# Feed-forward products as pairs of 64-row matmuls in two PSUM banks

## The chip, the cores and the metric

One core of a Trainium2 chip runs the kernel. The metric is the device time in microseconds from the first to the last instruction, the median of several runs. One more execution is recorded by the hardware profiler; all rows below come from it.

## What is computed

One layer of a hybrid encoder block in float32, 256 tokens of width 2048: a combined input projection, latent attention and a convolution branch, a gated merge, cross-attention to 256 memory tokens, a SwiGLU feed-forward of width 5632, and a final RMSNorm. The change touches only the feed-forward part:

```python
def rms_norm(x, g):
    xf = x.astype(jnp.float32)
    y = xf * lax.rsqrt(jnp.mean(xf * xf, axis=-1, keepdims=True) + EPS)
    return (y * g.astype(jnp.float32)).astype(x.dtype)

def swiglu(h, w_gate, w_up, w_down):
    return (jax.nn.silu(h @ w_gate) * (h @ w_up)) @ w_down
...
        x = x + swiglu(rms_norm(x, norm_ffn[l]), w_gate[l], w_up[l], w_down[l])
    return rms_norm(x, norm_final)
```

## The kernel before

The kernel is a hand-written program for each engine, synchronised by semaphores; nothing plans it at run time. All large products are done in split form: a float32 operand is a sum of two fp32r parts, high and low, and a product of two operands is three matmuls (low x high, high x low, high x high) that add into the same PSUM bank. The activations are kept transposed in SBUF as such pairs (crossT, actT: 128 rows of the contraction, 16 or 44 blocks, 256 tokens).

The weights come from memory in tiles of 128 rows x 2 blocks x 512 columns (512 KB). Tile t goes through a ring of four places: SyncE loads it into `raw` (`tile`, L259, waits until `split_lo` is done with the place's last tile), ScalarE rounds it to w_hi (`split_hi`, L717; it waits for the DMA and, for tile t, until TensorE is done with tile t - 4), VectorE subtracts to w_lo (`split_lo`, L1162), TensorE multiplies (`products`, L324). In the streams of ScalarE and VectorE the split of tile t + 4 stands at step t.

A chunk is 512 columns of the output for all 256 tokens. It lies in `acc`, two banks, one for each block b of 128 tokens. `products` does for one weight tile: for b in 0, 1, for each block k of the tile, three matmuls of 128 x 128 against 128 x 512. A full tile is thus 12 matmuls. A chunk of gate or up is 8 tiles, a chunk of down 24 tiles (four of them with one block: 264 matmuls). On the chunk's last tile the end of block 0 is signalled by `acc0_full`, the end of block 1 by `tile_done`, six matmuls later. On the first tile of a chunk the matmuls of block b wait for `acc_free[b]`.

The feed-forward stage has 11 pairs of chunks (gate, up), the first written out, ten in a loop (L689), then four chunks of down (L698). The counts are 176 x 12 = 2112 matmuls for gate and up and 4 x 264 = 1056 for down. ScalarE evicts a gate chunk with the silu (`silu_out`, L1103, the output silu_g is the first half of row_bc, so the profile calls it row_bc) ahead of its split of step 7. VectorE evicts an up chunk (`gated_up`, L1555: acc times rfac times silu_g, to `stage`) ahead of its split of step 14. After tile 1 of the next pair TensorE transposes `stage` (`turn_stage`, L354: eight 128x128 transposes in fp32 against the identity) and the two engines take the result apart into actT (`act_hi`, `act_lo`). VectorE evicts a down chunk by adding acc to the residual xs (L1593), ahead of its split of step 22; ScalarE then sums the squares (L748). The PSUM banks `sc` are used by the attention parts and are idle in the feed-forward stage.

In the attention part, at L452 and L457, scores are made in fp32: per head, 128-row products with 128 and 256 columns into bank sc[:, h], then the rope part with only 64 rows of contraction. The two heads' rope parts lie in partitions 0:64 and 64:128. An fp32 matmul call shows as two passes in the trace.

Of the kernel before, what the change touches and what calls it, by code (L numbers as in the profile page):

```python
# [23 lines left out]
ACT = mybir.ActivationFunctionType  # L24
ALU = mybir.AluOpType
# [3 lines left out]
P = 128  # L29
TOK = 256  # L30
NB = TOK // P
D = 2048
DK = D // P
CH = 512
# [5 lines left out]
D_FF = 5632  # L40
# [7 lines left out]
RING = 4  # L48
# [37 lines left out]
def program(nc, x, mem, positions, norm_mix, w_in, b_conv_in, norm_cq, w_uq, norm_ckv, w_ukv, w_dw,  # L86
# [15 lines left out]
    with ctx:  # L102
# [3 lines left out]
        def sem(name):  # L106
            return ctx.enter_context(nc.semaphore(name))
# [127 lines left out]
        silu_done = sem("silu_done")  # L235
        x_done = sem("x_done")
        table_loaded = sem("table_loaded")
        gained = sem("gained")
# [81 lines left out]
        def _(pe):  # L320
# [3 lines left out]
            def products(base, t, n_tiles, lhs, k0, kt, n, chunk):  # L324

                s = t % RING
                first, last = t == 0, t == n_tiles - 1
                pe.wait_ge(lo_done, base + (t + 1))
                for b in range(NB):
                    if first and not (isinstance(chunk, int) and chunk == 0):  # L330
                        pe.wait_ge(acc_free[b], chunk)
                    for k in range(kt):
                        hi = lhs[0][:, k0 + k, b * P:(b + 1) * P]
                        lo = lhs[1][:, k0 + k, b * P:(b + 1) * P]
                        whi = w_hi[:, s, k * n:(k + 1) * n]
# [5 lines left out]
                        ins = mm(o, hi, whi, start=False, stop=end)  # L341
                    if last and b == 0:
                        ins.then_inc(acc0_full, 1)
                ins.then_inc(tile_done, 1)
# [336 lines left out]
            for t in range(8):  # L681
                if t % 2 == 0:
                    operand_ready(Q_H + t // 2)
                products(T_I, t, 8, crossT, 2 * t, 2, CH, C_I)
                if t == 1:
                    turn_stage(Q_H + 3, 2 * (S_H + 4))
            for t in range(8):
                products(T_I + 8, t, 8, crossT, 2 * t, 2, CH, C_I + 1)
            with pe.Fori(1, D_FF // CH) as i:  # L689
                for t in range(8):  # L690
                    products(i * 16 + T_I, t, 8, crossT, 2 * t, 2, CH, 2 * i + C_I)
                    if t == 1:
                        turn_stage(i + (Q_I - 1), 2 * i + 2 * S_I)
                for t in range(8):
                    products(i * 16 + (T_I + 8), t, 8, crossT, 2 * t, 2, CH, 2 * i + (C_I + 1))


            def down(c, first):  # L698
                for t in range(24):
                    k, kt = down_tile(t)  # L700
                    if first and t == 22:
                        operand_ready(Q_I + 10)
                    products(c * 24 + T_J, t, 24, actT, k, kt, CH, c + C_J)
                    if first and t == 1:
                        turn_stage(Q_I + 10, 2 * (S_I + 11))

# [7 lines left out]
        def _(act):  # L714
            fn = nc.scalar.activation

            def split_hi(base, t, width=TW):  # L717

                s = t % RING
                act.wait_ge(raw_full[s], base * 4 + (16 * (t // RING) + 16))  # L720
                if not (isinstance(base, int) and base + t < RING):
                    act.wait_ge(tile_done, base + (t - RING + 1))
                fn(w_hi[:, s, 0:width], raw[:, s, 0:width], ACT.Copy).then_inc(hi_done, 1)  # L723
# [376 lines left out]
                x_update(c, False, T_H, Q_H, S_H, Z_H, R_FFN, "norm_ffn")  # L1100


            def silu_out(chunk, last_tile, n):  # L1103

                if not (isinstance(n, int) and n == 0):
                    act.wait_ge(stage_full, 2 * n + 2 * S_I)
                for b in range(NB):
                    acc_full(b, chunk, last_tile)
                    fn(silu_g[:, b, :], acc[:, b, :], ACT.Silu, scale=rfac[:, R_FFN, b:b + 1])\
                        .then_inc(silu_done, 1)  # L1110
                    act.wait_ge(silu_done, 2 * n + (b + 1))
                    act.sem_inc(acc_free[b], 1)

            def act_hi(n, count):
                for g in range(2):
                    turned_hi_part(g, count + (g + 1), [actT[0][:, cols(n * 4 + 2 * g, 2), :]])

            for t in range(16):
                if t == 7:
                    act.wait_ge(r_ready, R_FFN + 1)  # L1120
                    silu_out(C_I, T_I + 8, 0)
                split_hi(T_I, t + 4)
                if t == 1:
                    new_x_hi(3, crossT, "norm_ffn", 2 * (Q_H + 3))
                    load_table(ACT.Silu)
            with act.Fori(1, D_FF // CH) as i:
                for t in range(16):
                    if t == 7:
                        silu_out(2 * i + C_I, i * 16 + (T_I + 8), i)
                    split_hi(i * 16 + T_I, t + 4)  # L1130
                    if t == 1:
                        act_hi(i - 1, 2 * i + (2 * Q_I - 2))


            def down(c, first, end):
                for t in range(24):
                    if t + 4 < 24 or not end:
                        split_hi(c * 24 + T_J, t + 4, down_tile((t + 4) % 24)[1] * CH)
                    if first and t == 1:
                        act_hi(10, 2 * (Q_I + 10))  # L1140
                for b in range(NB):
                    act.wait_ge(x_done, 2 * c + (b + 1))
                    sum_squares(2 * c + (Z_J + b), R_FIN, b, c, xs[:, b, cols(c * CH, CH)])
# [15 lines left out]
        def _(dve):  # L1159
# [10 lines left out]
            def acc_full(b, chunk, last_tile):  # L1170
                if b == 0:
                    dve.wait_ge(acc0_full, chunk + 1)
                else:
                    dve.wait_ge(tile_done, last_tile)
# [377 lines left out]
                        new_x_lo(c - 1, "norm_ffn", 2 * c + (H_H - 2))  # L1552


            def gated_up(b, n, chunk, last_tile, free):  # L1555

                dve.wait_ge(turned, free)
# [11 lines left out]
            for t in range(16):  # L1569
                if t == 0:  # L1570
                    mean_square(R_FFN, D, 4, Z_H + 8)
                if t == 14:
                    dve.wait_ge(x_new, 8)
                    dve.wait_ge(r_ready, R_FFN + 1)
                for b in range(NB) if t == 14 else ():
                    gated_up(b, 0, C_I + 1, T_I + 16, 2 * (Q_H + 4))
                split_lo(T_I, t + 4)
                if t == 1:
                    new_x_lo(3, "norm_ffn", H_H + 6)
            with dve.Fori(1, D_FF // CH) as i:  # L1580
                for t in range(16):
                    for b in range(NB) if t == 14 else ():
                        gated_up(b, i, 2 * i + (C_I + 1), i * 16 + (T_I + 16), 2 * i + 2 * Q_I)
                    split_lo(i * 16 + T_I, t + 4)
                    if t == 1:
# [211 lines left out]
```

## Time and profile before

| what | value |
|---|---|
| median of 3 runs | 1701.45 us (1700.97 to 1701.63) |
| profiled execution | 1700.04 us, its span 1698.2 us |
| TensorE busy | 1679.2 us, 7808 matmuls |
| VectorE busy | 972.7 us |
| ScalarE busy | 814.0 us |
| feed-forward, gate and up | 958.5 to 1447.5 us of the span |
| feed-forward, down | 1447.5 to 1687.8 us |

PE is TensorE's matmuls, PEld its weight loads, DVE VectorE, ACT ScalarE, SP SyncE. A row of the timeline gives the start and the length in us, then engine, line, operation, output and inputs. A matmul's length is a modelled one from the start of its reading to its end, longer than the distance to the next matmul, which starts meanwhile. A group of instructions of one form that follow each other is one row with its count.

### The profile page before, as it was taken

How to read it: one execution, taken by the hardware profiler on the slowest of the kernel's cores; microseconds unless marked ns; L12 is line 12 of the kernel's file. 1: busy time of each engine (PE TensorE's matmuls, PEld its weight loads, DVE VectorE, ACT ScalarE, POOL GpSimd, SP SyncE). 2: the span in 40 equal slices, each digit the busy share in tenths (PEclk: the TensorE clock that was granted, in tenths of full speed). 3: DMA queues.
4: the chain of work that ended last, by engine and by line, in shares of the span. 5: the costliest groups of instructions: out<-in, count | busy, mean ns of one | idle time of the engine just before them, and what ended most of it. 6: DMA issues, size and time to landing. Idle time of an engine off the chain costs nothing.

```text
span 1698.2 us, 23828 instructions
## 1 busy us (share of the span) xinstructions
PE 1679.2 (99%) x7808; PEld 1393.2 (82%) x7808; DVE 972.7 (57%) x1154; ACT 814.0 (48%) x1061; POOL 88.0 (5%) x154
## 2 busy tenths in 40 slices
PE   8999999999999999999999999999999999999997
PEld 6888888888888888888778888888888888888886
DVE  5545777778886467554445645544444454554453
ACT  6555555556545444445445544444444444344343
POOL 4100100010000000000000000000000000000000
PEclk9999999999999999999999999999999999999999
DMA  6866555555566655554435566666666666565563
GB/s 214 273 195 170 170 164 152 166 155 167 173 210 186 197 174 179 193 187 148 135 124 186 186 187 190 192 188 188 182 184 197 195 188 187 197 211 186 183 212 124
DMA packets 161295, 309.64 MB, mean 182 GB/s; under 512 B 10323, under 2 KB 16577, under 8 KB 160992
## 3 DMA queue, kind: packets, MB, share of 16 engines
q1 hardware_dynamic: 159168, 302.55, 57.9%
q0 software_dynamic: 1776, 6.47, 1.0%
q8 instruction: 27, 0.44, 0.1%
q14 instruction: 20, 0.16, 0.0%
q10 hardware_dynamic: 304, 0.01, 0.0%
HBM read 306.89 MB, written 2.10 MB: 182 GB/s over the span
## 4 chain that ended last, share of the span: by engine, by line
PE 98%; ACT 1%; DMA 0%; DVE 0%; issue 0%; ACTq 0%; POOL 0%; DVEq 0%
PE acc L339 29%; PE acc L341 29%; PE acc L340 29%; PE tp L351 3%; PE sc L631 1%; PE acc L530 1%; PE sc L452 1%; PE acc L532 1%; PE acc L531 1%; PE ov L650 0%; PE acc L510 0%; PE acc L512 0%; PE acc L511 0%; PE ov L476 0%; PE xt L650 0%; PE sc L457 0%
## 5 line engine op out<-in xcount | busy, mean ns | idle before, releaser
L1167 DVE TENSOR_TENSOR w_lo<-raw,w_hi 128x1024 fp32r<-128x1024 f32 (+3 forms) x592 | 709.9, 1204 | 606.1 <-ACT w_hi L723 602.3
L723 ACT ACTIVATE w_hi<-raw 128x1024 fp32r<-128x1024 f32 (+3 forms) x592 | 606.8, 1027 | 786.8 <-PE acc L341 751.7
L339 PE MATMUL acc<-w_hi,crossT 128*128 128x512 f32 x832 | 327.4, 394 | 0.0
L341 PE MATMUL acc<-w_hi,crossT 128*128 128x512 f32 x832 | 324.1, 390 | 0.0
L340 PE MATMUL acc<-w_lo,crossT 128*128 128x512 f32 x832 | 323.9, 389 | 0.0
L339 PE MATMUL acc<-w_hi,mixT 128*128 128x512 f32 x800 | 318.2, 398 | 2.9 <-DVE w_lo L1167 2.4
L341 PE MATMUL acc<-w_hi,mixT 128*128 128x512 f32 x800 | 312.8, 391 | 0.0
L340 PE MATMUL acc<-w_lo,mixT 128*128 128x512 f32 x800 | 312.6, 391 | 0.0
L339 PEld LDWEIGHTS acc<-w_hi,crossT 128*128 128x128 f32 x832 | 156.2, 188 | 32.8 <-issue 0.7
L341 PEld LDWEIGHTS acc<-w_hi,crossT 128*128 128x128 f32 x832 | 156.2, 188 | 32.7
L340 PEld LDWEIGHTS acc<-w_lo,crossT 128*128 128x128 f32 x832 | 156.3, 188 | 32.2 <-issue 0.7
L339 PEld LDWEIGHTS acc<-w_hi,mixT 128*128 128x128 f32 x800 | 150.8, 188 | 37.4 <-issue 6.4
L341 PEld LDWEIGHTS acc<-w_hi,mixT 128*128 128x128 f32 x800 | 150.7, 188 | 32.0
L340 PEld LDWEIGHTS acc<-w_lo,mixT 128*128 128x128 f32 x800 | 151.0, 189 | 29.4
L339 PE MATMUL acc<-w_hi,actT 128*128 128x512 f32 x352 | 137.0, 389 | 0.0
L341 PE MATMUL acc<-w_hi,actT 128*128 128x512 f32 x352 | 136.9, 389 | 0.0
L340 PE MATMUL acc<-w_lo,actT 128*128 128x512 f32 x352 | 136.9, 389 | 0.0
L1291 DVE SCALAR_TENSOR_TENSOR conv<-uT,wdwT,conv (+1 forms) x240 | 118.2, 492 | 19.5 <-DVE conv L1291 16.7
L341 PEld LDWEIGHTS acc<-w_hi,actT 128*128 128x128 f32 x352 | 66.1, 188 | 13.8
L339 PEld LDWEIGHTS acc<-w_hi,actT 128*128 128x128 f32 x352 | 66.1, 188 | 13.7
L340 PEld LDWEIGHTS acc<-w_lo,actT 128*128 128x128 f32 x352 | 66.1, 188 | 13.6
L339 PE MATMUL acc<-w_hi,oT 128*128 128x512 f32 x128 | 51.0, 399 | 0.1
(224 smaller groups left out, 1235.1 us busy)
## 6 DMA issues: line engine op xcount, KB each, us to landing
raw<-in_w_in_dram SPq DMA_DIRECT2D x104, 512.0 KB, 3.8
raw<-in_w_gate_dram SPq DMA_DIRECT2D x88, 512.0 KB, 4.5
raw<-in_w_up_dram SPq DMA_DIRECT2D x88, 512.0 KB, 3.7
raw<-in_w_down_dram SPq DMA_DIRECT2D x80, 512.0 KB, 4.0
raw<-in_w_kv_mem_dram SPq DMA_DIRECT2D x64, 512.0 KB, 3.8
raw<-in_w_o_dram SPq DMA_DIRECT2D x32, 512.0 KB, 3.9
raw<-in_w_q_mem_dram SPq DMA_DIRECT2D x32, 512.0 KB, 3.6
raw<-in_w_o_mem_dram SPq DMA_DIRECT2D x32, 512.0 KB, 3.6
```

What stands on the lines that cost most here:

```text
L339: mm(o, lo, whi, start=first and k == 0, stop=False)
L340: mm(o, hi, wlo, start=False, stop=False)
L341: ins = mm(o, hi, whi, start=False, stop=end)
L351: ins = turn(tp[:, bank, j * P:(j + 1) * P], src, ident[:, :])
L452: mm(sc[:, h, at:at + keys], qnT[:, h, qs:qs + P], knT[:, h, 0:keys], start=qs == 0, stop=False, skip_group_check=True)
L530: mm(o, lo, w_hi[:, s, k * n:(k + 1) * n], start=first and k == 0, stop=False)
L531: mm(o, hi, w_lo[:, s, k * n:(k + 1) * n], start=False, stop=False)
L532: ins = mm(o, hi, w_hi[:, s, k * n:(k + 1) * n], start=False, stop=last and k == kt - 1)
L631: ins = mm(sc[:, 0, b * TOK:(b + 1) * TOK], memqT[:, k, b * P:(b + 1) * P], memKT[:, cols(h * 4 + k, 1), :].rearrange("p o t -> p (o t)"), ...
L723: fn(w_hi[:, s, 0:width], raw[:, s, 0:width], ACT.Copy).then_inc(hi_done, 1)
L1167: V.tensor_tensor(w_lo[:, s, 0:width], raw[:, s, 0:width], w_hi[:, s, 0:width].bitcast(F32), ALU.subtract).then_inc(lo_done, 1)
L1291: ins = V.scalar_tensor_tensor(out=a, in0=u, scalar=wt, in1=a, op0=ALU.mult, op1=ALU.add)
```

## The change

In the whole feed-forward stage `products` is replaced by `half_products`: each 128-row matmul becomes two of 64 rows, the upper half of the contraction into acc[:, b], the lower into sc[:, b]; the two are issued one behind the other. An output is then the sum of two banks. At eviction ScalarE copies the half in sc to SBUF (`half_copy`, into silu_g for a gate chunk, into `stage` for the others), VectorE adds acc to it in place (`gate_sum`, `gated_up`, and in `down`), and that addition signals `acc_free`. The silu then runs in place in SBUF behind ScalarE's split of step 7, the product with rfac and silu_g (`gated`) in SBUF behind VectorE's split of step 14, and the addition to xs as a second addition. In the down chunks `half_copy` stands behind ScalarE's split of step 23.

```diff
+            def half_products(base, t, n_tiles, lhs, k0, kt, chunk):
+
+                s = t % RING
+                first, last = t == 0, t == n_tiles - 1
+                pe.wait_ge(lo_done, base + (t + 1))
+                for b in range(NB):
+                    if first:
+                        pe.wait_ge(acc_free[b], chunk)
+                    for k in range(kt):
+                        hi, lo = lhs[0][:, k0 + k, b * P:(b + 1) * P], lhs[1][:, k0 + k, b * P:(b + 1) * P]
+                        whi, wlo = w_hi[:, s, k * CH:(k + 1) * CH], w_lo[:, s, k * CH:(k + 1) * CH]
+                        for n, (a, w) in enumerate(((lo, whi), (hi, wlo), (hi, whi))):
+                            for bank, rows in ((acc, slice(0, 64)), (sc, slice(64, P))):
+                                ins = mm(bank[:, b, :], a[rows, :], w[rows, :], start=first and k == 0 and n == 0,
+                                         stop=last and k == kt - 1 and n == 2)
                     if last and b == 0:
                         ins.then_inc(acc0_full, 1)
                 ins.then_inc(tile_done, 1)
...
             with pe.Fori(1, D_FF // CH) as i:
                 for t in range(8):
-                    products(i * 16 + T_I, t, 8, crossT, 2 * t, 2, CH, 2 * i + C_I)
+                    half_products(i * 16 + T_I, t, 8, crossT, 2 * t, 2, 2 * i + C_I)
                     if t == 1:
                         turn_stage(i + (Q_I - 1), 2 * i + 2 * S_I)
...
-            def silu_out(chunk, last_tile, n):
-
-                if not (isinstance(n, int) and n == 0):
-                    act.wait_ge(stage_full, 2 * n + 2 * S_I)
+            def half_copy(dst, chunk, last_tile):
+
                 for b in range(NB):
                     acc_full(b, chunk, last_tile)
-                    fn(silu_g[:, b, :], acc[:, b, :], ACT.Silu, scale=rfac[:, R_FFN, b:b + 1])\
+                    fn(dst[:, b, :], sc[:, b, :], ACT.Copy).then_inc(half_out, 1)
+
+            def silu_out(chunk):
+
+                for b in range(NB):
+                    act.wait_ge(acc_free[b], chunk + 1)
+                    fn(silu_g[:, b, :], silu_g[:, b, :], ACT.Silu, scale=rfac[:, R_FFN, b:b + 1])\
                         .then_inc(silu_done, 1)
-                    act.wait_ge(silu_done, 2 * n + (b + 1))
-                    act.sem_inc(acc_free[b], 1)
...
             with act.Fori(1, D_FF // CH) as i:
                 for t in range(16):
                     if t == 7:
-                        silu_out(2 * i + C_I, i * 16 + (T_I + 8), i)
+                        act.wait_ge(stage_full, 2 * i + 2 * S_I)
+                        half_copy(silu_g, 2 * i + C_I, i * 16 + (T_I + 8))
+                    if t == 15:
+                        act.wait_ge(turned, 2 * i + 2 * Q_I)
+                        half_copy(stage, 2 * i + (C_I + 1), i * 16 + (T_I + 16))
                     split_hi(i * 16 + T_I, t + 4)
+                    if t == 7:
+                        silu_out(2 * i + C_I)
...
                         split_hi(c * 24 + T_J, t + 4, down_tile((t + 4) % 24)[1] * CH)
                     if first and t == 1:
                         act_hi(10, 2 * (Q_I + 10))
+                    if t == 23:
+                        if first:
+                            act.wait_ge(turned, 2 * (Q_I + 11))
+                        act.wait_ge(x_done, 2 * c)
+                        half_copy(stage, c + C_J, c * 24 + (T_J + 24))
...
+            def gated_up(b, n):
+
+                dve.wait_ge(half_out, 4 * n + (b + 3))
+                V.tensor_tensor(stage[:, b, :], acc[:, b, :], stage[:, b, :], ALU.add).then_inc(acc_free[b], 1)
+
+            def gated(b, n, chunk):
+
+                dve.wait_ge(acc_free[b], chunk + 1)
                 dve.wait_ge(silu_done, 2 * n + (b + 1))
-                acc_full(b, chunk, last_tile)
-                V.scalar_tensor_tensor(out=stage[:, b, :], in0=acc[:, b, :], scalar=rfac[:, R_FFN, b:b + 1],
+                V.scalar_tensor_tensor(out=stage[:, b, :], in0=stage[:, b, :], scalar=rfac[:, R_FFN, b:b + 1],
                                        in1=silu_g[:, b, :], op0=ALU.mult, op1=ALU.mult).then_inc(stage_full, 1)
-                dve.wait_ge(stage_full, 2 * n + (2 * S_I + b + 1))
-                dve.sem_inc(acc_free[b], 1)
+
+            def gate_sum(b, n):
+
+                dve.wait_ge(half_out, 4 * n + (b + 1))
+                V.tensor_tensor(silu_g[:, b, :], acc[:, b, :], silu_g[:, b, :], ALU.add).then_inc(acc_free[b], 1)
...
             with dve.Fori(1, D_FF // CH) as i:
                 for t in range(16):
+                    for b in range(NB) if t == 6 else ():
+                        gate_sum(b, i)
                     for b in range(NB) if t == 14 else ():
-                        gated_up(b, i, 2 * i + (C_I + 1), i * 16 + (T_I + 16), 2 * i + 2 * Q_I)
+                        gated_up(b, i)
                     split_lo(i * 16 + T_I, t + 4)
+                    for b in range(NB) if t == 14 else ():
+                        gated(b, i, 2 * i + (C_I + 1))
...
                         acc_full(b, c + C_J, c * 24 + (T_J + 24))
-                        V.tensor_tensor(xs[:, b, cols(c * CH, CH)], acc[:, b, :], xs[:, b, cols(c * CH, CH)],
+                        dve.wait_ge(half_out, 2 * c + (4 * (D_FF // CH) + b + 1))
+                        V.tensor_tensor(stage[:, b, :], acc[:, b, :], stage[:, b, :], ALU.add).then_inc(acc_free[b], 1)
+                        dve.wait_ge(acc_free[b], c + (C_J + 1))
+                        V.tensor_tensor(xs[:, b, cols(c * CH, CH)], stage[:, b, :], xs[:, b, cols(c * CH, CH)],
                                         ALU.add).then_inc(x_done, 1)
-                        dve.wait_ge(x_done, 2 * c + (b + 1))
-                        dve.sem_inc(acc_free[b], 1)
```

## Rows read from the trace of the kernel before

**Rows 1.** The page: busy time, the clock granted in 40 slices, the chain.

```profile
PE 1679.2 (99%) x7808; PEld 1393.2 (82%) x7808; DVE 972.7 (57%) x1154; ACT 814.0 (48%) x1061; POOL 88.0 (5%) x154
...
PEclk9999999999999999999999999999999999999999
...
PE 98%; ACT 1%; DMA 0%; DVE 0%; issue 0%; ACTq 0%; POOL 0%; DVEq 0%
```

**Rows 2.** Groups by line, TensorE, feed-forward stage: count, busy us, mean ns, idle.

```profile
L339 PE MATMUL acc<-w_hi,crossT 128*128 128x512 f32 x704 | 274.9, 391 | 0.0
...
L339 PE MATMUL acc<-w_hi,actT 128*128 128x512 f32 x352 | 137.0, 389 | 0.0
```

**Rows 3.** Timeline, TensorE, down products: the first and the last of 15.

```profile
1579.66 0.39 PE L339 MATMUL acc<-w_hi,actT 128*128 128x512 f32 x1
...
1582.84 0.39 PE L341 MATMUL acc<-w_hi,actT 128*128 128x512 f32 x1
```

**Rows 4.** Timeline, products of 384 columns: the first and the last of 12.

```profile
237.08 0.33 PE L531 MATMUL acc<-w_lo,cqT 128*128 128x384 f32 x1
...
238.98 0.33 PE L530 MATMUL acc<-w_hi,cqT 128*128 128x384 f32 x1
```

**Rows 5.** Timeline, TensorE, scores: whole stretch, then windows that cut the half passes.

```profile
218.36 0.38 PE L452 MATMUL sc<-knT,qnT 128*128 128x256 f32 x1
...
218.67 0.93 PE L457 MATMUL sc<-krT,qrT 64*128 64x128 f32 x8
219.53 0.50 PE L339 MATMUL acc<-w_hi,mixT 128*128 128x512 f32 x1
219.86 0.40 PE L340 MATMUL acc<-w_lo,mixT 128*128 128x512 f32 x1
...
218.67 0.38 PE L457 MATMUL sc<-krT,qrT 64*128 64x128 f32 x2
...
218.67 0.49 PE L457 MATMUL sc<-krT,qrT 64*128 64x128 f32 x4
...
219.00 0.59 PE L457 MATMUL sc<-krT,qrT 64*128 64x256 f32 x3
```

**Rows 6.** Timeline, TensorE, the transposes of `stage` between products.

```profile
1052.68 0.39 PE L341 MATMUL acc<-w_hi,crossT 128*128 128x512 f32 x1
1052.91 1.03 PE L351 MATMUL tp<-ident,stage 128*128 128x128 f32 x8
...
1054.02 0.39 PE L340 MATMUL acc<-w_lo,crossT 128*128 128x512 f32 x1
```

**Rows 7.** Timeline, the end of a gate chunk and its eviction.

```profile
1068.55 0.39 PE L341 MATMUL acc<-w_hi,crossT 128*128 128x512 f32 x1
...
1068.98 0.69 ACT L1109 ACTIVATE row_bc<-acc,rfac 128x512 f32<-128x512 f32 x1 [0.30 <-PE acc L341]
...
1069.91 0.39 PE L341 MATMUL acc<-w_hi,crossT 128*128 128x512 f32 x1
1069.91 0.19 PEld L339 LDWEIGHTS acc<-w_hi,crossT 128*128 128x128 f32 x1
```

**Rows 8.** Groups by line, ScalarE and VectorE, feed-forward stage.

```profile
L736 ACT ACTIVATE actT<-tp 128x512 f32 x20 | 10.7, 588 | 0.0
...
L1593 DVE TENSOR_TENSOR xs<-acc,xs 128x512 f32<-128x512 f32 x4 | 2.8, 692 | 10.2 <-PE acc L341 10.2
```

**Rows 9.** Timeline, the end of the first down chunk.

```profile
1508.04 0.39 PE L341 MATMUL acc<-w_hi,actT 128*128 128x512 f32 x1
...
1508.52 1.06 ACT L723 ACTIVATE w_hi<-raw 128x1024 fp32r<-128x1024 f32 x1 [1.66 <-PE acc L341]
```

**Rows 10.** Timeline, behind the last matmul.

```profile
1687.56 0.39 PE L341 MATMUL acc<-w_hi,actT 128*128 128x512 f32 x1
...
1687.98 0.69 DVE L1593 TENSOR_TENSOR xs<-acc,xs 128x512 f32<-128x512 f32 x1 [0.67 <-PE acc L341]
1688.70 0.63 ACT L748 ACTIVATE junk<-xs 128x512 f32<-128x512 f32 x1 [0.64 <-DVE xs L1593]
```

More of the change, by code:

```diff
@@ L234, in program @@
         x_new = sem("x_new")
-        silu_done = sem("silu_done")
+        silu_done, half_out = sem("silu_done"), sem("half_out")
         x_done = sem("x_done")
@@ L341, in products @@
                         ins = mm(o, hi, whi, start=False, stop=end)
+                    if last and b == 0:
+                        ins.then_inc(acc0_full, 1)
+                ins.then_inc(tile_done, 1)
+            def half_products(base, t, n_tiles, lhs, k0, kt, chunk):
[12 more added lines that the diff above has]
+                                         stop=last and k == kt - 1 and n == 2)
                     if last and b == 0:
@@ L683, in _ @@
                     operand_ready(Q_H + t // 2)
-                products(T_I, t, 8, crossT, 2 * t, 2, CH, C_I)
+                half_products(T_I, t, 8, crossT, 2 * t, 2, C_I)
                 if t == 1:
@@ L687, in _ @@
             for t in range(8):
-                products(T_I + 8, t, 8, crossT, 2 * t, 2, CH, C_I + 1)
+                half_products(T_I + 8, t, 8, crossT, 2 * t, 2, C_I + 1)
             with pe.Fori(1, D_FF // CH) as i:
                 for t in range(8):
-                    products(i * 16 + T_I, t, 8, crossT, 2 * t, 2, CH, 2 * i + C_I)
+                    half_products(i * 16 + T_I, t, 8, crossT, 2 * t, 2, 2 * i + C_I)
                     if t == 1:
@@ L694, in _ @@
                 for t in range(8):
-                    products(i * 16 + (T_I + 8), t, 8, crossT, 2 * t, 2, CH, 2 * i + (C_I + 1))
+                    half_products(i * 16 + (T_I + 8), t, 8, crossT, 2 * t, 2, 2 * i + (C_I + 1))
             def down(c, first):
@@ L702, in down @@
                         operand_ready(Q_I + 10)
-                    products(c * 24 + T_J, t, 24, actT, k, kt, CH, c + C_J)
+                    half_products(c * 24 + T_J, t, 24, actT, k, kt, c + C_J)
                     if first and t == 1:
@@ L1119, in _ @@
                 if t == 7:
+                    half_copy(silu_g, C_I, T_I + 8)
+                if t == 15:
+                    act.wait_ge(turned, 2 * (Q_H + 4))
+                    half_copy(stage, C_I + 1, T_I + 16)
+                split_hi(T_I, t + 4)
+                if t == 7:
                     act.wait_ge(r_ready, R_FFN + 1)
-                    silu_out(C_I, T_I + 8, 0)
-                split_hi(T_I, t + 4)
+                    silu_out(C_I)
                 if t == 1:
@@ L1128, in _ @@
                     if t == 7:
-                        silu_out(2 * i + C_I, i * 16 + (T_I + 8), i)
+                        act.wait_ge(stage_full, 2 * i + 2 * S_I)
+                        half_copy(silu_g, 2 * i + C_I, i * 16 + (T_I + 8))
+                    if t == 15:
+                        act.wait_ge(turned, 2 * i + 2 * Q_I)
+                        half_copy(stage, 2 * i + (C_I + 1), i * 16 + (T_I + 16))
                     split_hi(i * 16 + T_I, t + 4)
+                    if t == 7:
+                        silu_out(2 * i + C_I)
                     if t == 1:
@@ L1574, in _ @@
                     dve.wait_ge(r_ready, R_FFN + 1)
+                for b in range(NB) if t == 6 else ():
+                    gate_sum(b, 0)
                 for b in range(NB) if t == 14 else ():
-                    gated_up(b, 0, C_I + 1, T_I + 16, 2 * (Q_H + 4))
+                    gated_up(b, 0)
                 split_lo(T_I, t + 4)
+                for b in range(NB) if t == 14 else ():
+                    gated(b, 0, C_I + 1)
                 if t == 1:
@@ L1581, in _ @@
                 for t in range(16):
+                    for b in range(NB) if t == 6 else ():
+                        gate_sum(b, i)
                     for b in range(NB) if t == 14 else ():
-                        gated_up(b, i, 2 * i + (C_I + 1), i * 16 + (T_I + 16), 2 * i + 2 * Q_I)
+                        gated_up(b, i)
                     split_lo(i * 16 + T_I, t + 4)
+                    for b in range(NB) if t == 14 else ():
+                        gated(b, i, 2 * i + (C_I + 1))
                     if t == 1:
```

2 lines of the change are left out of this document (removed).

## Prediction

> **What bounds the kernel now.** I read the page first: TensorE is busy for 1679.2 of 1698.2 us, its clock is at full level in every slice, and it holds 98% of the chain that ended last [rows 1]. So the time is the number of matmuls times their pitch, plus whatever makes TensorE wait. In the feed-forward stage the groups of instructions by line show no idle time in front of any matmul group: 3 lines x 704 with crossT and 3 x 352 with actT, 3168 products of 128x512 [rows 2]. The reported 390 ns of one is a modelled length that overlaps the next one, so I take the pitch from the timeline: 14 steps from 1579.66 to 1582.84 us are 0.227 us each [rows 3]. 3168 x 0.227 = 719 us; 12 groups of 8 transposes add 10. That is the whole stage: it has no slack and no waits, and anything added to TensorE's path is paid in full. The 384-wide products take 0.173 (11 steps in 1.90 us [rows 4]): 128 columns less save 0.054 us, 0.42 ns each, one column per cycle of 2.4 GHz. So of the 0.227 us, 0.213 are columns and 0.0135 a fixed part.
>
> **Pitch of a pair.** Each product of 128 rows becomes two of 64 rows on the two halves of the array, into acc and sc: 6336 matmuls and 6336 weight loads for the same arithmetic. A half streams the same 512 columns, so a pair can at best cost what one product costs now. Whether the two run side by side is shown by the rope part of the attention scores, which already does exactly this (rows 0:64 and 64:128, banks sc 0 and sc 1). In its timeline two matmuls start within the same 0.01 us, the next two 0.11 later than the first work could begin (4 done at 218.67 + 0.49), and with 256 columns the third starts at 219.00 + 0.59 - 0.38 = 219.21, about 0.22 after the first of its pair [rows 5]. For whole-array fp32 the transposes give 0.109 for 128 columns [rows 6], so about 0.216 for 256. So a pair costs what a single one costs, within a rounding of 1 to 3 ns. What this does not show is the 1-pass fp32r form at a full column per cycle and its 13.5 ns fixed part (in fp32 a column takes two cycles, and of the 0.109 only 2 ns are fixed). Bounds: the fixed part disappears for halves, 0.227 - 0.011 = 0.216, or is paid once for each half, 0.227 + 0.0135 = 0.2405. The nearest row (the half pairs) says "the same", so I take +1 ns: 3168 x 0.001 = **+3 us**, with -35 and +43 us as ends.
>
> In the Trainium skill, the page "TensorE: Matmul & The Clock Gate" (Part 3, The mechanism) models a pack as one matmul's duration plus about 4 ns per further tile. No 512-column pair is in this trace; as an estimate by that page the term would be 3168 x 0.004 = 13 us in place of 3, and the total 1736.
>
> **Changing between whole array and halves.** The last full pass of the scores starts at 218.36, the half passes last 2 x 0.11 + 2 x 0.22 = 0.66, so without any loss the next two full products would start at 219.24 and 219.47. The second one starts at 219.86 [rows 5]: 0.39 to 0.40 us for an excursion, 0.20 per change. In the changed stage the excursion goes the other way: the transposes of turn_stage are whole-array. They come 12 times (one in the first gate chunk, ten in the loop, one in the first down chunk), plus one entry into the stage: 25 changes x 0.20 = 5.0 us. Today the same transposes lose next to nothing: 1052.68 + 0.227 + 8 x 0.109 + 0.227 = 1054.01 against 1054.02 seen [rows 6]. **+4.9 us.**
>
> **Freeing the accumulator, gate and up chunks.** Before, one instruction reads acc[b] and frees it. Take M, the start of the last matmul of block 0 of a chunk (1068.55). ScalarE starts at M + 0.43, and TensorE's weight load for the next chunk's block 0 comes at M + 1.36 [rows 7]; the present silu of 0.69 ends in time by 0.2. After the change ScalarE copies the sc half (0.59 us, as the actT copy of the same 128x512 out of PSUM), and only then VectorE adds (0.69 us, as the x add of the same shape) [rows 8], with 0.03 us from one engine to the next (1687.98 + 0.69 to 1688.70 [rows 10]). So the bank is free at M + 0.43 + 0.59 + 0.03 + 0.69 + 0.03 = M + 1.77, 0.41 after the weight load wanted it. A weight load may be 0.12 late for free, since it needs no more than 0.109 of the 0.227. Stall: 0.30 us (0.29 rounded up). Block 1's copy starts 1.36 later and its add is over at M + 3.14, when its weight load, itself pushed to M + 2.72 + 0.30, may wait until 3.14: no second stall. There are 11 gate-to-up, 10 up-to-gate and one up-to-down boundaries: 22 x 0.30 = **+6.6 us**. VectorE and ScalarE are otherwise free then; what queues behind their waits is split_lo(t+4) and split_hi(t+4), due three tiles or 8 us later. The silu in SBUF and the product with rfac come after the bank is free: on no path, except that the next turn_stage needs both some 5.4 us after the chunk's end. I find them done at 4.5 (add 1.8, split_lo 1.25, two products of 0.75 at most). If that cover failed, each of 11 turn_stages would wait for the excess.
>
> **Freeing it in the down chunks.** Here half_copy stands behind split_hi(27), and that waits for the last tile of the chunk. With M1 the start of the chunk's very last matmul (1508.04), the split starts at M1 + 0.48 and takes 1.06 [rows 9]; then copy of block 0 to M1 + 2.15, add to 2.87, seen at 2.90, while the next chunk's weight load wants to go at M1 + 0.00. Less the free 0.12: 2.78 us of stall, at 3 boundaries **+8.3 us**. Block 1 follows within its 1.36 us. The splits of tiles 26 and 27 end by M1 + 7.6, their use is at 8.4 and later.
>
> **Tail.** Before, the last x add runs from M1 + 0.42 for 0.69 [rows 10], over at 1.11. After: copy to 1.01, VectorE still has block 0's second add until 1.09, then two adds of 0.69 with 0.03 each in front, over at 2.53. **+1.4 us.**
>
> Sum: 3 + 4.9 + 6.6 + 8.3 + 1.4 = 24.4 us. The profiled execution took 1700.0, so it would take 1724.4; the median lies 1.4 above that execution, which gives **1726 us**.
>
> **Rivals.**
> 1. *The fixed part is paid by every half* (the two halves share what costs 13.5 ns between matmuls). For it: nothing in the trace has fp32r halves, and two loads and two matmuls now pass where one each did. Against: in the rope pairs it was not doubled [rows 5]. Pitch 0.2405, +43 us in place of +3; the boundary stalls shrink a little. About 1765.
> 2. *The halves hide the weight change*, and the fixed part goes. The page "TensorE: Matmul & The Clock Gate" in the Trainium skill gives 512/2.4 + 2.5 ns, 216 ns, as back-to-back gap (Back-to-back issue gap), and says that a weight load overlaps running matmuls only where the row group differs (Part 3); by that rule the change would gain. Against: a load starts with the running whole-array matmul already now (both at 1069.91 [rows 7]), and both halves change weights at the same moment, so neither covers the other. Worked out from rows: -35 + 21.2 = -14 us at full effect, 1688; at half effect 1705. This is how it ends faster: it decides once the pair's pitch falls below 0.227 - 21.2/3168 = 0.2203.
> 3. *The pairs don't run side by side* in this form, because two banks would now take a full column per cycle each, twice what the rope pairs wrote. Pitch 0.454, about +720 us: 2440. A part of it (one half delayed by some tens of ns) would land between.
> 4. *More stalls than counted*: three gaps of 2.8 us in the down chunks let the clock fall to 1.2 GHz (no fall is seen within the stage now [rows 1]); if each then slowed one tile of 2.7 us to half speed, +8 us; or transposes wait for the later products. About 1735 to 1745.
>
> **How the numbers follow.** Forecast (pitch 0.226 to 0.230): 0.58, its own range 1721 to 1735. Rival 1: 0.14. Rival 2: 0.14, of which 0.09 faster by over 0.2%, 0.03 within it and 0.02 slower. Rival 3: 0.06. Rival 4: 0.08. A measurement of this kernel can tell about 0.2% (3.4 us) from no change. Faster 0.09, within 0.2% 0.04 (the 0.03 and a hundredth for stalls that vanish with an unchanged pitch), slower 0.87. The range 1704 to 1770 takes in the forecast, rivals 1 and 4 and the weak end of rival 2, and leaves out the serial case and the clear gain.
>
> **What the profile after would show.** Right: some 6336 half matmuls of 64 rows, two starting together and the next two 0.228 later; about 0.3 us of TensorE waiting for VectorE at each of 22 boundaries, 2.8 at three; 0.2 more in front of and behind each group of 8 transposes. Wrong: a pitch near 0.240 or 0.216 (rival 1 or 2), second halves starting 0.2 behind the first (rival 3), a digit below 9 in the clock's row (rival 4), or boundaries without idle time, which would mean that the copy or the add is shorter than the rows taken for them, or that TensorE's wait is later than its weight load.

## The result

The changed kernel takes 1725.7 us (median of 4 runs, 1724.8 to 1727.6) against 1701.2 us before on the same chip: a ratio of 1.0148, 95% interval 1.0136 to 1.0160. It is slower by 24.5 us; 1726 was forecast. The profiled execution took 1724.8 us, its span is 1723.0.

The page of the kernel after, to be held against [rows 1]: TensorE's share falls by one point although it now has 10976 matmuls, and the chain goes through VectorE and ScalarE at times.

```profile
span 1723.0 us, 30227 instructions
...
PE 1692.7 (98%) x10976; PEld 1398.0 (81%) x10976; DVE 1003.7 (58%) x1206; ACT 840.2 (49%) x1113; POOL 87.2 (5%) x154
...
PE 95%; ACT 2%; DVE 1%; DMA 1%; issue 1%; ACTq 0%; POOL 0%; DVEq 0%; SPq 0%
```

The timeline of TensorE inside a tile, to be held against [rows 3] and [rows 5]: two halves start together, the next two 0.227 us later (7 steps in 1.59 us). The pairs run side by side in fp32r as the rope parts did in fp32.

```profile
1399.83 0.39 PE L359 MATMUL acc<-w_hi,crossT 64*128 64x512 f32 x1
1399.84 0.39 PE L359 MATMUL sc<-w_hi,crossT 64*128 64x512 f32 x1
1400.06 0.39 PE L359 MATMUL acc<-w_lo,crossT 64*128 64x512 f32 x1
...
1401.42 0.39 PE L359 MATMUL acc<-w_lo,crossT 64*128 64x512 f32 x1
```

An up-to-gate boundary, all engines, the counterpart of [rows 7] (gate-to-up ones look the same). M is 1048.26. The copy starts at M + 0.43, the addition at M + 1.06; the weight load that could have gone at 1049.62 goes at 1050.07, M + 1.81. Of these 0.45 us the free 0.12 of the prediction goes off, and 0.33 is lost:

```profile
1048.26 0.39 PE L359 MATMUL sc<-w_hi,crossT 64*128 64x512 f32 x1
...
1048.69 0.60 ACT L1126 ACTIVATE stage<-sc 128x512 f32<-128x512 f32 x1 [0.30 <-PE sc L359]
...
1049.32 0.69 DVE L1595 TENSOR_TENSOR stage<-acc,stage 128x512 f32<-128x512 f32 x1 [2.39 <-ACT stage L1126]
...
1049.62 0.39 PE L359 MATMUL acc<-w_hi,crossT 64*128 64x512 f32 x1
...
1050.07 0.18 PEld L359 LDWEIGHTS acc<-w_hi,crossT 64*128 64x128 f32 x1 [0.48 <-DVE stage L1595]
```

The first down boundary, counterpart of [rows 9]: the chunk's last matmul starts at 1521.01, the split runs first, then two copies (one row), then the addition, and the next chunk begins at 1523.90. The two steps that are stretched come to 2.89 + 0.34, which is 2.77 more than two steps of 0.227.

```profile
1521.01 0.39 PE L359 MATMUL acc<-w_hi,actT 64*128 64x512 f32 x1
...
1521.50 1.06 ACT L742 ACTIVATE w_hi<-raw 128x1024 fp32r<-128x1024 f32 x1 [1.66 <-PE sc L359]
1522.47 1.06 ACT L1126 ACTIVATE stage<-sc 128x512 f32<-128x512 f32 x2
1523.15 0.69 DVE L1646 TENSOR_TENSOR stage<-acc,stage 128x512 f32<-128x512 f32 x1 [4.76 <-ACT stage L1126]
...
1523.90 0.49 PE L359 MATMUL acc<-w_hi,actT 64*128 64x512 f32 x1 [2.50 <-DVE stage L1646]
```

The transposes of `stage`, counterpart of [rows 6]. From the last pair in front to the second pair behind there are 1057.12 - 1055.45 = 1.67 us; two steps of 0.227 and eight of 0.109 are 1.33, so 0.35 is lost (before: 0.01).

```profile
1055.45 0.39 PE L359 MATMUL acc<-w_hi,crossT 64*128 64x512 f32 x1
...
1055.77 1.09 PE L370 MATMUL tp<-ident,stage 128*128 128x128 f32 x8
1056.79 0.50 PE L359 MATMUL acc<-w_hi,crossT 64*128 64x512 f32 x1
...
1057.12 0.39 PE L359 MATMUL acc<-w_lo,crossT 64*128 64x512 f32 x1
```

And one thing that no step of the sum had: behind the second of the three long gaps the clock fell. The busy time by stretches (columns: stretch and length in us, then TensorE, weight loads, VectorE, ScalarE, GpSimd, then the granted clock, the share of the DMA engines and GB/s) shows the gap, the stretch behind it, and the one after that:

```profile
1583.90:1586.40 2.50, 0.15 (x2) 0.00 (x0) 0.69 (x1) 2.03 (x3) 0.00 (x0) 1.00 0.51 179
1586.40:1590.90 4.50, 4.48 (x26) 3.56 (x28) 4.23 (x5) 1.45 (x4) 1.22 (x1) 0.62 0.00 0
1590.90:1595.40 4.50, 4.50 (x42) 4.07 (x40) 3.88 (x3) 2.12 (x2) 1.19 (x1) 1.00 0.54 167
```

A clock of 0.62 over this stretch is most of it at 1.2 GHz: in the timeline seven steps in a row take 0.427 us each, and the stretch as a whole costs 1.6 us. The page's row of the clock, which the prediction named as the sign, does not show it: it has 9 in every fortieth (43 us) of the stage, and an 8 only in the last one, where the clock fell behind the last product.

**Where the 24.8 us of the span went.** The feed-forward stage, from the start of its first matmul to the start of its last, went from 729.05 to 751.60 us, +22.6. The steps of the timeline in it, taken one by one, give: 22 boundaries of gate and up 7.5 us (19 of 0.33, two of 0.39, one of 0.49), three down boundaries 8.1 (2.77, 2.64, 2.66), 12 groups of transposes and the entry 4.3, the low clock 1.6, and the pitch 1.0 (the steady steps, those beside waits, transposes and the low clock, are 0.2272 us on average against 0.2269). Behind the last matmul it is 1.9 us more, ahead of the stage 0.3.

### The profile page after: what moved, and what is told of

It reads as the page before. It is cut to its first block, busy times and chain, and to the rows that moved or that the text cites. A ratio compares the mean times of both kernels' runs of the same rounds, so it can differ in the third digit from the quotient of the medians.

```text
span 1723.0 us, 30227 instructions
## 1 busy us (share of the span) xinstructions
PE 1692.7 (98%) x10976; PEld 1398.0 (81%) x10976; DVE 1003.7 (58%) x1206; ACT 840.2 (49%) x1113; POOL 87.2 (5%) x154
## 4 chain that ended last, share of the span: by engine, by line
PE 95%; ACT 2%; DVE 1%; DMA 1%; issue 1%; ACTq 0%; POOL 0%; DVEq 0%; SPq 0%
PE acc L359 39%; PE acc L339 15%; PE acc L341 15%; PE acc L340 15%; PE tp L370 3%; PE sc L359 2%; PE sc L650 1%; PE acc L549 1%; PE sc L471 1%; PE acc L551 1%; PE acc L550 1%; ACT stage L1126 1%; PE ov L669 0%; DVE row_bc L1607 0%; DVE stage L1595 0%
## 5 line engine op out<-in xcount | busy, mean ns | idle before, releaser
L359 PE MATMUL acc<-w_hi,crossT 64*128 64x512 f32 x1408 | 441.1, 389 | 1.5 <-DVE stage L1595 0.2
L359 PE MATMUL sc<-w_hi,crossT 64*128 64x512 f32 x1408 | 441.0, 389 | 0.0
L359 PEld LDWEIGHTS acc<-w_hi,crossT 64*128 64x128 f32 x1408 | 259.1, 184 | 67.1 <-DVE stage L1595 5.0
L359 PE MATMUL acc<-w_lo,crossT 64*128 64x512 f32 x704 | 272.1, 387 | 0.0
L359 PE MATMUL sc<-w_lo,crossT 64*128 64x512 f32 x704 | 272.1, 387 | 0.0
L359 PEld LDWEIGHTS sc<-w_hi,crossT 64*128 64x128 f32 x1408 | 259.1, 184 | 1.5
L359 PE MATMUL acc<-w_hi,actT 64*128 64x512 f32 x704 | 218.3, 389 | 7.4 <-DVE stage L1646 7.2
L359 PE MATMUL sc<-w_hi,actT 64*128 64x512 f32 x704 | 218.3, 389 | 0.0
L359 PEld LDWEIGHTS acc<-w_lo,crossT 64*128 64x128 f32 x704 | 129.6, 184 | 24.8
L359 PE MATMUL sc<-w_lo,actT 64*128 64x512 f32 x352 | 136.7, 388 | 0.0
L359 PE MATMUL acc<-w_lo,actT 64*128 64x512 f32 x352 | 136.6, 388 | 0.0
```

Of the source, the lines that this page charges most:

```text
L359: ins = mm(bank[:, b, :], a[rows, :], w[rows, :], start=first and k == 0 and n == 0, stop=last and k == kt - 1 and n == 2)
```

## Experiments

Each ratio is to the kernel before on the same chip; where none is given, the time is that of one execution. The kernel before took 1700.6 to 1701.5 us on these chips, so a difference between two changed kernels can be off by some 0.8 us where they ran on different chips.

**1. The new eviction alone, without halves.** The last matmul of each block of a chunk goes to `sc`, everything behind it is as in the changed kernel:

```diff
-                        for n, (a, w) in enumerate(((lo, whi), (hi, wlo), (hi, whi))):
-                            for bank, rows in ((acc, slice(0, 64)), (sc, slice(64, P))):
-                                ins = mm(bank[:, b, :], a[rows, :], w[rows, :], ...)
+                        end = last and k == kt - 1
+                        mm(acc[:, b, :], lo, whi, start=first and k == 0, stop=False)
+                        mm(acc[:, b, :], hi, wlo, start=False, stop=end)
+                        ins = mm(sc[:, b, :] if end else acc[:, b, :], hi, whi, start=end, stop=end)
```

> Whole-array products as before (the same count of matmuls, no halves, no change between whole array and halves), but the last matmul of each block of a chunk goes to the second bank and the chunk is evicted as in the changed kernel: ScalarE copies the second bank, VectorE adds. Theory (most of the loss is the later freeing of the banks): 22 boundaries x 0.33 us + 3 down boundaries x 2.7 + 1.5 to 2 at the end = 17 us above the kernel before, about 1718, and 1.6 more if the clock falls after one of the long gaps. Rival (the loss is in the half matmuls, their doubled instructions or their loads): nothing of it is here, 1701 to 1704.

Measured: 1722.5 us, ratio 1.0128 (1.0113 to 1.0144), 21.9 us above the kernel before. The mechanism is confirmed: the boundaries have the same stretched steps as with halves (0.445 + 0.335 us in place of twice 0.227; 2.88, 2.75 and 2.75 in the down chunks), and none of what is lost at the boundaries needs half matmuls. The forecast of 1718 was 4 us too low, because here the clock fell at all three long gaps, 4.5 us in all, and not behind one. The pitch tells something too: between the waits the whole-array products of this run take 0.2272 us on average, as the pairs do in the changed kernel.

```profile
1520.00:1522.20 2.20, 2.20 (x7) 1.71 (x6) 2.17 (x4) 1.45 (x4) 0.00 (x0) 0.50 0.00 0
1583.90:1586.90 3.00, 3.00 (x8) 2.32 (x7) 2.84 (x5) 1.45 (x4) 0.37 (x1) 0.50 0.00 0
1648.70:1651.70 3.00, 3.00 (x8) 2.26 (x7) 2.86 (x4) 1.13 (x4) 1.08 (x1) 0.50 0.00 0
```

**2. The copy of the down chunks ahead of the split.**

```diff
                 for t in range(24):
+                    if t == 23:
+                        ...
+                        half_copy(stage, c + C_J, c * 24 + (T_J + 24))
                     if t + 4 < 24 or not end:
                         split_hi(c * 24 + T_J, t + 4, down_tile((t + 4) % 24)[1] * CH)
-                    if t == 23:
-                        ...
-                        half_copy(stage, c + C_J, c * 24 + (T_J + 24))
```

> The changed kernel with the copy of the down chunks placed ahead of ScalarE's split of step 23 instead of behind it. Theory: the three gaps of 2.64 to 2.77 us shrink to the 0.33 of the other boundaries, 7.1 us less, and the 1.6 us at half clock behind one of the gaps go too: 1717 to 1719. Rival (the gap is set by VectorE's two additions per block or by block 1, not by the split ahead of the copy): at most 1 to 2 us less, 1724.

Measured: 1717.3 us, ratio 1.0096 (1.0080 to 1.0111), 8.4 less than the changed kernel. The timeline at the first down boundary: the next chunk begins 0.60 us after 1522.60 in place of 2.89, and ScalarE's split follows the copies. No stretch of the stage is at the low clock any more. So the long gap was the one split of 1.06 us and the missed head start of 1.36 us, not the additions. Of the three boundaries one still costs 0.49 us and two 0.33.

```profile
1521.75 0.60 ACT L1126 ACTIVATE stage<-sc 128x512 f32<-128x512 f32 x1 [0.32 <-PE sc L359]
...
1522.46 0.69 DVE L1646 TENSOR_TENSOR stage<-acc,stage 128x512 f32<-128x512 f32 x1 [1.71 <-ACT stage L1126]
...
1522.60 0.39 PE L359 MATMUL sc<-w_hi,actT 64*128 64x512 f32 x1
...
1523.20 0.50 PE L359 MATMUL acc<-w_hi,actT 64*128 64x512 f32 x1 [0.22 <-DVE stage L1646]
...
1523.52 1.05 ACT L742 ACTIVATE w_hi<-raw 128x1024 fp32r<-128x1024 f32 x1
```

**3 and 4. The price of leaving the halves.** The same extra transpose in each of the 22 gate and up chunks, once in the changed kernel and once in the kernel before:

```diff
+                    if t == 4:
+                        turn(xt[:, 0:P], ident[:, :], ident[:, :])
```

> The changed kernel with one more whole-array transpose of the identity into an unused bank in each of the 22 gate and up chunks (nobody reads it, nothing waits for it). Theory (each change between halves and whole array costs 0.17 to 0.20 us): 22 x (0.109 + 0.34) = 9.9 us more, 1735.6. Rival (the changes are free and the transposes' 1.22 us are something else, a wait for stage or for the bank): 22 x 0.11 = 2.4 us more, 1728.

> The control: the kernel before with the same 22 extra transposes. Both theories: 22 x (0.109 + 0.01) = 2.6 us more, 1704. If it costs 9 us here too, the price is that of a transpose between products and not of changing to halves.

Measured: with halves 1736.6 us (ratio 1.0212, 1.0198 to 1.0226), 10.8 more than the changed kernel without them; whole 1703.6 us (ratio 1.0019, 1.0009 to 1.0028), 2.9 more. In the timeline with halves (the first rows below) the stretch 1020.93 to 1021.84 is 0.91 us, less two steps of 0.227 and 0.109 for the transpose: 0.35 lost per excursion, 7.7 us in 22. With the transposes' 2.4 that is 10.1; the rest of the 10.8 lies in the steady steps (0.2275 us in place of 0.2272). In the control (the last rows) the same place loses 0.007 (0.257 + 0.313). It is the change between halves and whole array that costs, 0.35 there and back. How it divides between the two ways no run shows cleanly; at the entry into the stage, which goes one way only, the two steps are 0.09 and 0.11 us longer than 0.227, 0.20 together.

```profile
1020.93 0.39 PE L359 MATMUL acc<-w_hi,crossT 64*128 64x512 f32 x1
...
1021.25 0.33 PE L716 MATMUL xt<-ident 128*128 128x128 f32 x1
1021.50 0.49 PE L359 MATMUL acc<-w_hi,crossT 64*128 64x512 f32 x1
...
1021.84 0.39 PE L359 MATMUL acc<-w_lo,crossT 64*128 64x512 f32 x1
```

```profile
1017.38 0.39 PE L341 MATMUL acc<-w_hi,crossT 128*128 128x512 f32 x1
1017.61 0.27 PE L697 MATMUL xt<-ident 128*128 128x128 f32 x1
1017.64 0.47 PE L339 MATMUL acc<-w_hi,crossT 128*128 128x512 f32 x1
1017.95 0.40 PE L340 MATMUL acc<-w_lo,crossT 128*128 128x512 f32 x1
```

**5. Three upper halves, then three lower ones.** Is it the alternating order that lets pairs run side by side?

```diff
-                        for n, (a, w) in enumerate(((lo, whi), (hi, wlo), (hi, whi))):
-                            for bank, rows in ((acc, slice(0, 64)), (sc, slice(64, P))):
+                        for bank, rows in ((acc, slice(0, 64)), (sc, slice(64, P))):
+                            for n, (a, w) in enumerate(((lo, whi), (hi, wlo), (hi, whi))):
```

> The changed kernel with the six half matmuls of a block in another order: the three of the upper half, then the three of the lower, in place of alternating. Theory (two halves run side by side only if they follow each other directly, since matmuls start in order): the third upper one runs beside the first lower one and the third lower beside the next first upper, so 4 slots of 0.227 us in place of 3, the feed-forward products take 958 us in place of 719, about 1960 to 1970 in all. Rival (TensorE takes the halves out of order, as it takes weight loads ahead): unchanged, 1726.

Measured: 1727.7 us in one execution, 2 us above the changed kernel's median: the clock fell behind two of its long gaps in place of one, 1.6 us more, and the 22 boundaries of gate and up cost 8.0 in place of 7.5. The 240 us that my theory adds are not there; it was wrong and the rival right. Although the program has three acc matmuls and then three sc matmuls, the timeline shows them in pairs, acc and sc by turns, 0.01 us apart:

```profile
1030.15 0.40 PE L359 MATMUL acc<-w_hi,crossT 64*128 64x512 f32 x1
1030.16 0.40 PE L359 MATMUL sc<-w_hi,crossT 64*128 64x512 f32 x1
1030.39 0.38 PE L359 MATMUL acc<-w_lo,crossT 64*128 64x512 f32 x1
1030.40 0.38 PE L359 MATMUL sc<-w_lo,crossT 64*128 64x512 f32 x1
```

**6 and 7. How far does that reach?** All six of a block's upper halves before the six lower ones, and (except in a chunk's first and last tile) all twelve of a tile. The loops over bank and rows move outward accordingly.

> The changed kernel with all six half matmuls of the upper half of a block first, then the six of the lower half. The order three and three cost nothing (1727.7), and its trace shows an upper and a lower one starting within 0.01 us of each other. Theory (each half of the array takes its next matmul from the queue by itself, past those that wait for the other half, as far as the queue reaches; rows elsewhere show TensorE's queue some 17 matmuls long): unchanged, 1726 to 1728. Rival (the reach is just a few instructions): between 1727 and 2200, with starts of upper and lower halves apart.

> The same with all twelve of the upper half of a tile (both blocks) first, then the twelve of the lower half, except in a chunk's first and last tile, where it is six and six. Theory of the reach: if it covers 12 matmuls with their 12 loads, unchanged, 1726 to 1728; if it ends between 6 and 12, the lower half starts late in each tile and the time grows by up to some hundred us, while six and six stays at 1727.

Measured: 1755.1 us with six, 2002.4 us with twelve. Neither is as the wide reach had it. The queue's length is not the reach: in the trace before, TensorE's sequencer works out the wait for the next chunk's bank at 1066.18 us, and that chunk's first matmul starts at 1070.14, 17 steps of 0.227 later. Six and six at the start of a chunk: the first lower half starts with the third upper one, when three upper ones have not started. From then on both halves of the array are busy; only where everything has to be waited for (22 + 3 boundaries and 12 groups of transposes) most of the skew of three slots, 0.68 us, is lost: the timeline has 0.67 us more at a boundary and 0.62 at a group of transposes, 25 x 0.67 + 12 x 0.62 = 24 of the 29 us above the changed kernel. Another 4.5 are the clock, which fell at all three long gaps here, for 6.1 us in all against 1.6.

```profile
1054.27 0.50 PE L359 MATMUL acc<-w_hi,crossT 64*128 64x512 f32 x1
1054.61 0.39 PE L359 MATMUL acc<-w_lo,crossT 64*128 64x512 f32 x1
1054.84 0.39 PE L359 MATMUL acc<-w_hi,crossT 64*128 64x512 f32 x1
1054.84 0.50 PE L359 MATMUL sc<-w_hi,crossT 64*128 64x512 f32 x1
```

Twelve and twelve: acc starts at 1060.30, the first lower half at 1062.25 with the ninth upper one, again with three not started (the row of 1061.56, not shown, stands for two matmuls), and the next tile's upper half begins only when the lower twelve are down to three as well, at 1064.21. A tile takes 3.91 us in place of 2.72.

```profile
1060.30 0.49 PE L356 MATMUL acc<-w_hi,crossT 64*128 64x512 f32 x1
...
1062.25 0.39 PE L356 MATMUL acc<-w_hi,crossT 64*128 64x512 f32 x1
1062.25 0.49 PE L356 MATMUL sc<-w_hi,crossT 64*128 64x512 f32 x1
...
1064.21 0.49 PE L356 MATMUL acc<-w_hi,crossT 64*128 64x512 f32 x1
```

**8. Both banks freed at the same time.** Experiment 2, and VectorE takes acc out without waiting for ScalarE's copy of sc; the sum is made in SBUF afterwards (for a down chunk: xs + acc, then + stage). TensorE waits for both engines. The copy of a gate chunk now goes to `stage` too. The cut shows the gate chunks:

```diff
-                dve.wait_ge(half_out, 4 * n + (b + 1))
-                V.tensor_tensor(silu_g[:, b, :], acc[:, b, :], silu_g[:, b, :], ALU.add).then_inc(acc_free[b], 1)
+                acc_full(b, chunk, last_tile)
+                V.tensor_copy(silu_g[:, b, :], acc[:, b, :]).then_inc(acc_free[b], 1)
+                dve.wait_ge(acc_free[b], chunk + 1)
+                dve.wait_ge(half_out, 4 * n + (b + 1))
+                V.tensor_tensor(silu_g[:, b, :], silu_g[:, b, :], stage[:, b, :], ALU.add).then_inc(gate_ready, 1)
```

> The copy of the down chunks ahead of the split, and in all chunks the two banks are freed by the two engines at the same time: ScalarE copies sc to stage as before, VectorE copies acc to SBUF (or adds it to xs in the down chunks) without waiting for that copy, and adds the two in SBUF later. TensorE waits for both. Theory (the boundary's 0.33 us is the addition standing behind the copy): free at M + 0.43 + 0.69 + 0.03 = M + 1.15 against the 1.36 that the weight load leaves, no idle time at 25 boundaries, 25 x 0.33 = 8.2 us less than with the copy moved alone (1717.3), and 0.7 less at the end: 1708.5 to 1710. Rival (the longer work of VectorE, one more addition per block, makes a split or stage late): 1715 to 1720.

Measured: 1706.1 us, ratio 1.0032 (1.0020 to 1.0044), 11.2 less than experiment 2 and some 3 us more than expected: the 25 boundaries had cost 8.8 us and not 8.2 (four of them 0.4 to 0.5 each), and the steady steps are 0.2268 us again in place of 0.2272, which is 1.2 us. The timeline has copy and copy overlapping, and no step of TensorE at a chunk boundary is longer than any other:

```profile
1049.13 0.60 ACT L1130 ACTIVATE stage<-sc 128x512 f32<-128x512 f32 x1 [0.76 <-PE sc L363]
...
1049.20 0.68 DVE L1599 COPY row_bc<-acc 128x512 f32<-128x512 f32 x1
```

**9. Transposes as halves too.** Experiment 8, and 11 of the 12 groups of transposes are pairs of 64 rows, upper rows to bank 0 of tp and lower ones to bank 1. Nothing has to be added here, since each half turns its own rows. TensorE's waits for `stage` and `tp` stand one pair earlier:

```diff
+                for j in range(8):
+                    k, b = j // 2, j % 2
+                    for h, rows in enumerate((slice(0, 64), slice(64, P))):
+                        ins = turn(tp[:, h, j * 64:(j + 1) * 64], stage[rows, b, k * P:(k + 1) * P], ident[rows, rows])
+                        if j == 7:
+                            ins.then_inc(turned, 1)
```

> The run before with the 11 groups of transposes of stage made of halves as well: 64 rows of each block into bank 0 of tp and 64 into bank 1, in pairs, so that TensorE stays in halves from the second tile of the stage on; the two engines take them out by halves. Theory (0.35 us per excursion, and 8 whole transposes of 0.109 become 8 pairs of some 0.056): 11 x 0.35 + 11 x 0.43 = 8.6 us less, about 1701, as fast as the kernel before. Rival (a pair of 64-column transposes is bound by the starting of its four instructions and not by columns, or the drain is one of fp32r to fp32 and stays): 0 to 4 us less, 1705 to 1709.

Measured: 1698.6 us (median of 11 runs), ratio 0.9988 (0.9979 to 0.9997): 2.2 us faster than the kernel before. It is 7.5 less than experiment 8. The runs of the two kernels do not overlap (the slowest of this one took 1699.2, the fastest of the kernel before 1699.7), but the gain is small. The timeline: 1052.51 to 1053.53 is 1.01 to 1.02 us, less two steps 0.56 for sixteen half transposes, 0.07 a pair and not 0.056, which is why it is 7.5 and not 8.6. A whole transpose streams 128 columns, a half one 64 (128x128 and 64x64 in the rows), so a pair is shorter than the whole, unlike a pair of products, where both halves stream all 512.

```profile
1052.51 0.39 PE L371 MATMUL acc<-w_hi,crossT 64*128 64x512 f32 x1
...
1052.74 0.66 PE L397 MATMUL tp<-ident,stage 64*128 64x64 f32 x16
1053.21 0.47 PE L371 MATMUL acc<-w_hi,crossT 64*128 64x512 f32 x1
...
1053.53 0.39 PE L371 MATMUL acc<-w_lo,crossT 64*128 64x512 f32 x1
```

The products bring nothing here: the steady step is 0.2269 us, as in the kernel before. The gain is that of the transposes, 11 x (0.88 - 0.56) = 3.5 us, less 0.4 for entering the halves and one excursion, less 0.9 behind the last matmul.

## Why the prediction was right

The forecast was 1726 and the result 1725.7, but that it came so close is luck: two groups of misses cancelled. Step by step, in the order of the sum:

- **Pitch of a pair**: forecast +3 us, found +1.0, and 0 once the waits are gone (experiments 8 and 9: 0.2268 and 0.2269). The row of the rope pairs said "the same", and the 1 ns on top was rounding. The 1.0 that was found is no price of the halves either: it lies in single steps of 0.236 us, 143 of them in place of 58, and the average is the same in experiment 1 with whole-array products. The fixed 13.5 ns are neither doubled (rival 1) nor hidden (rival 2): the half-array form pays them once per pair. The estimate by the page "TensorE: Matmul & The Clock Gate" of the Trainium skill (Part 3, 4 ns per further tile, 13 us) would have been 12 us too high: the two halves do start 0.00 to 0.01 us apart in most pairs and up to 0.06 in the others, but in a steady stream the next pair isn't moved by it.
- **Changing between halves and whole array**: forecast 4.9, found 4.3. An excursion costs 0.35, not 0.39 to 0.40; experiments 3 and 4 show that it belongs to the change and not to the transposes.
- **Gate and up boundaries**: forecast 6.6, found 7.5. VectorE's end to TensorE's weight load takes 0.06 us and not the 0.03 that I took from a VectorE-to-ScalarE row; three boundaries beside loop starts and ends cost 0.06 to 0.16 more. Block 1 has no second stall, as worked out.
- **Down boundaries**: forecast 8.3, found 8.1, by the mechanism named (experiment 2).
- **Tail**: forecast 1.4, found 1.9: relative to the last matmul, the last sum of squares starts 1.46 later (2.60 in place of 1.14) and the first output transfer 1.26 later (4.18 in place of 2.92); the other 0.7 come up until the last transfer has landed. Why they do was not looked into.
- **Left out of the sum**: the clock, 1.6 us. It was in rival 4, with 8 us at three gaps. The mechanism is there, it struck behind one gap in this trace, and its size is 1.6 and not 2.7 per gap. The forecast put it at nothing.

Terms in all: forecast 24.4, found 24.8 in the span. Pitch and changes were 2.6 us too high together, clock, boundaries and tail 2.8 too low together; ahead of the stage it was 0.3 more. Rival 3 (the halves do not run side by side) did not happen: with a pitch of 0.227 us both banks take all 512 columns in the time in which one took them before. That the extra split behind the waits, the silu and the product cost nothing held too: no weight tile was late in the feed-forward stage.

## What to carry to other kernels

Splitting a full 128-row product into two 64-row ones bought no time on TensorE: the pair costs what the one did (0.227 us for 512 columns), and the price is the second bank and its eviction. If two banks have to be emptied, let both engines start at the same time and add in SBUF; the length of the chain from the last matmul to the freed bank, against the time until the bank is wanted again (here 1.36 us, given by the second block), decides the stall, and an unrelated split ahead of the copy in the queue counts in that chain in full. Halves paid here only in the transposes, where each half has half the columns to stream and the results need no adding (0.56 in place of 0.88 us for eight), and only because the engine then stays in halves: leaving and coming back costs 0.35 us, more than the 0.32 that eight transposes gain.

## What was not expected of the hardware

The two halves of the array take their matmuls out of program order. The lower half starts work that stands behind up to three upper-half matmuls that have not started (with their weight loads), in experiment 5 at next to no loss. With twelve in a row the reach is exceeded and a tile takes 3.91 us. Whether three matmuls or, say, six instructions with the loads are what limits it, no run tells apart. A signal on the last matmul of the program order is thus not, by itself, a sign that the other half's matmuls before it are over; in the changed kernel's trace, from 985.6 to 1004 us, the lower half runs some 0.02 us ahead of the upper one, so that at seven ends of tiles the matmul that carries `tile_done` starts and ends before its partner (the first of them in the rows below). It did no harm: the partner ends at 988.02, and the split that waits for the signal starts at 988.13. No run tested a longer lead.

```profile
987.62 0.39 PE L359 MATMUL sc<-w_hi,crossT 64*128 64x512 f32 x1
987.63 0.39 PE L359 MATMUL acc<-w_hi,crossT 64*128 64x512 f32 x1
```

The clock: the long gaps at the down boundaries, which cost 2.6 to 2.8 us, came with a fall to 1.2 GHz in 1 of 3 places in the changed kernel, in 1 of 3 with the extra transposes, in 2 of 3 with runs of three, and in 3 of 3 with whole-array products (experiment 1), at 1.3 to 1.6 us each. With runs of six and of twelve the gaps are 0.7 us longer, and it was 3 of 3 both times, at 1.6 to 2.8 us each. The fall begins between 0.9 us before the gap's end and 1.6 us behind it. Boundaries that cost 0.3 to 0.5 us never had one. What decides among the long ones is open.
